# 512 columns per matmul in the down products of the first two feed-forward layers

## The reference

```python
def conv_ffn(h, w_in, dw, w_out):
    u = causal_dwconv(h @ w_in, dw)
    gate, val = u[..., :D_FF], u[..., D_FF:]
    return (jax.nn.silu(gate) * val) @ w_out      # D_FF = 2816
...
x = x + conv_ffn(rmsnorm(x, norm_ffn_g[layer]), ffn_w_in[layer], ffn_dw[layer], ffn_w_out[layer])
```

## Time and profile before

| | |
|---|---|
| median of three runs | 2604.6 us |
| the profiled execution | 2604.33 us, of which the span of the trace is 2602.5 us |
| granted TensorE clock, mean of the span | 0.986 |
| PE busy | 2506.9 us (96%), 25266 matmuls |
| PEld busy | 2367.6 us (91%), 25266 weight loads |
| DVE, ACT, POOL busy | 52%, 43%, 38% |

### The profile page before, as it was taken

One profiled execution on the slowest core, in us unless ns is written; L12 is line 12 of the kernel. 1 busy time (PEld: TensorE's weight loads), 2 busy tenths in 40 slices (PEclk: granted clock), 3 DMA queues, 4 the chain that ended last, 5 costly groups with the idle time before them and its releaser, 6 DMA issues.

```text
span 2602.5 us, 62231 instructions
## 1 busy us (share of the span) xinstructions
PE 2506.9 (96%) x25266; PEld 2367.6 (91%) x25266; DVE 1340.9 (52%) x2035; ACT 1122.6 (43%) x1652; POOL 995.2 (38%) x488
## 2 busy tenths in 40 slices
PE   6999898999999999998999999999999999999998
PEld 6888796997999999977989999999998769999998
DVE  7657554613477741798533677612143344455521
ACT  7834455454444433334534344433244444444422
POOL 3324220461444444325322444444443104444442
PEclk8899999999999999999999999999999999999999
DMA  4221001251232233323212322233222103322232
GB/s 147 74 65 59 2 1 63 82 194 38 94 97 95 91 102 100 130 65 105 90 65 65 97 94 91 92 111 114 88 93 69 49 1 97 97 89 97 96 99 74
DMA packets 62180, 219.43 MB, mean 84 GB/s; under 512 B 6752, under 2 KB 9184, under 8 KB 61408
## 3 DMA queue, kind: packets, MB, share of 16 engines
q1 hardware_dynamic: 58880, 207.76, 24.4%
q10 hardware_dynamic: 3168, 9.75, 1.1%
HBM read 213.29 MB, written 4.19 MB: 84 GB/s over the span
## 4 chain that ended last, share of the span: by engine, by line
PE 83%; DVE 8%; issue 6%; ACT 2%; POOL 1%; DMA 0%; DVEq 0%; POOLq 0%; ACTq 0%
PE psum L571 70%; DVE psum L2698 5%; PE psum L713 3%; PE psum L721 2%; PE psum L1072 1%; PE psum L1021 1%; PE psum L1251 1%; POOL wl L520 1%; PE psum L1290 1%; DVE psum L2267 1%; PE psum L1253 0%; ACT wh L1382 0%; PE psum L683 0%; PE psum L1278 0%; PE psum L690 0%
## 5 line engine op out<-in xcount | busy, mean ns | idle before, releaser
L520 POOL TENSOR_TENSOR wl<-raw,wh 128x1024 fp32r<-128x1024 f32 x388 | 949.0, 2455 | 1464.0 <-ACT wh L1382 1463.6
L571 PE MATMUL psum<-acth,wh 128*128 128x256 f32 x3792 | 763.8, 283 | 20.6 <-DVE actl L2789 8.2
L571 PE MATMUL psum<-actl,wh 128*128 128x256 f32 x3792 | 753.9, 281 | 0.0
L571 PE MATMUL psum<-acth,wl 128*128 128x256 f32 x3792 | 753.3, 280 | 0.0
L1382 ACT ACTIVATE wh<-raw 128x1024 fp32r<-128x1024 f32 x388 | 407.1, 1056 | 625.1 <-PE psum L571 601.4
L571 PEld LDWEIGHTS psum<-acth,wh 128*128 128x128 f32 x3792 | 582.7, 189 | 38.1 <-issue 30.2
L571 PEld LDWEIGHTS psum<-acth,wl 128*128 128x128 f32 x3792 | 581.7, 189 | 0.0
L571 PEld LDWEIGHTS psum<-actl,wh 128*128 128x128 f32 x3792 | 581.5, 189 | 0.0
L2628 DVE TENSOR_TENSOR cu<-psum,rstd 128x512 f32<-128x512 f32 x132 | 91.1, 690 | 236.9 <-PE psum L571 219.6
L571 PE MATMUL psum<-hidh,wh 128*128 128x256 f32 x1056 | 210.0, 277 | 0.0
L571 PE MATMUL psum<-hidh,wl 128*128 128x256 f32 x1056 | 209.5, 277 | 0.0
(11 more groups left out here) (442 smaller groups left out, 4048.3 us busy)
## 6 DMA issues: line engine op xcount, KB each, us to landing
raw<-in_weights SPq DMA_DIRECT2D x388, 512.0 KB, 3.3
xt<-in_x SPq DMA_DIRECT2D x4, 512.0 KB, 5.4
xt<-in_x ACTq DMA_DIRECT2D x1, 2048.0 KB, 9.3
out_x<-xt SPq DMA_DIRECT2D x6, 256.0 KB, 2.3
mem<-in_mem ACTq DMA_DIRECT2D x1, 1024.0 KB, 11.0
memn<-memh ACTq DMA_DIRECT2D x1, 1024.0 KB, 7.0
memn<-meml ACTq DMA_DIRECT2D x1, 1024.0 KB, 10.0
memh<-memn ACTq DMA_DIRECT2D x1, 1024.0 KB, 4.7
```

Of the source, the lines that this page charges most:

```text
L520: pool.tensor_tensor(wl[:, s, :], raw[:, s, :], wh[:, s, :].bitcast(F32), ALU.subtract).then_inc(split_done, 1)
L571: ins = pe.matmul(out[:, n:n + HALF], w, m[:, n:n + HALF], start=first and n == 0, stop=last and n + HALF >= out.shape[1])
```

## The change

`product` gets the parameter `width`, 256 unless given, in place of the constant HALF. `down` gives width=T, so each pair of operands is one matmul of 512 columns instead of two of 256. Nothing else is changed: same blocks, order, banks, waits and slots. `dense`, `tile` and `last_down` keep 256.

```diff
-            def product(out, slot, b, hi, lo, start, stop, rows=slice(0, P)):
+            def product(out, slot, b, hi, lo, start, stop, rows=slice(0, P), width=HALF):
 
                 w_h, w_l = wh[rows, slot, b * P:(b + 1) * P], wl[rows, slot, b * P:(b + 1) * P]
                 for w, m, first, last in ((w_h, hi, start, False), (w_h, lo, False, False), (w_l, hi, False, stop)):
-                    for n in range(0, out.shape[1], HALF):
-                        ins = pe.matmul(out[:, n:n + HALF], w, m[:, n:n + HALF], start=first and n == 0,
-                                        stop=last and n + HALF >= out.shape[1])
+                    for n in range(0, out.shape[1], width):
+                        ins = pe.matmul(out[:, n:n + width], w, m[:, n:n + width], start=first and n == 0,
+                                        stop=last and n + width >= out.shape[1])
                 return ins
...
                             mm = product(bank[(t0 + s) % 4][:, :], (u0 + j) % SLOTS, k % BLOCKS,
-                                         hi[:, k, :], lo[:, k, :], k == 0, k == FT - 1)
+                                         hi[:, k, :], lo[:, k, :], k == 0, k == FT - 1, width=T)
```

## The result

The changed kernel is slower: 2616.1 us against 2605.8 (medians of 13 runs each), a ratio of 1.0032 with a 95% interval from 1.0019 to 1.0045. The two medians differ by 10.3 us; the ratio, which uses all the runs, stands for about 8 us, with 5 to 12 inside the interval. The profiled execution took 2611.83 us, with a span of 2610.0, which is 7.5 us more than before.

The account below looks back on a forecast made before the run. The prediction took TensorE to bound the kernel, busy 96% of the span. Its one term, 1056 x (226.7 ns minus the 512-column step), came to 0 against the profiled 2604.33 us, giving 2604.5 us, range 2593 to 2608.5.

Parts of the forecast that it names:

- TensorE sets the span: Whole kernel: PE busy 96% of the span, 83% of the last chain, so its pace reaches the end nearly undiminished.
- Nothing waited differently: Down products: slot and bank are still released when the last column is through, which is the same column.
- the slots and POOL kept up: Down products: POOL, with 57.5 us of work in 119.6, would keep up even with a stage 10 us shorter.
- the clock stayed at 1.00: Down products: the granted clock stays at 1.00, the 2.4 GHz level; otherwise the forecast is wrong.
- The stages right before and behind kept their steps: Stages around the down products: they keep 256 columns and their pace, unchanged to the tenth of a microsecond.
- PEld's busy time: Down products: the weight loads' busy time falls by half without any gain in the span.
- the price of a 512-column matmul: Down products: excess goes with columns, so 512 columns step in 226.7 ns; the term 1056 x 0 is 0, chance 0.66.
- rival 2: Down products: late hand-over between long matmuls at every step, +6.7 us, to 2611.3 us; chance 0.10.
- The bound that I allowed: Down products: upper bound on the 512-column step, 233 ns from L1254 in the attention, 6.7 us slower.
- a weight load which is not hidden: Third layer's attention: such a load lies in the 256- and 512-column forms alike and drops out of their difference.
- Rival 1: Down products: a fixed time per instruction, halved by the change; 7.0 us saved (2597.6) or 10.6 (2594.0); chance 0.24.
- The formula: Down products: a warm gap of N / 2.4 + 2.5 ns, 215.8 ns at 512 columns, would give 11.5 us; not built on.

Follow-up runs that it names:

- e10_all_moved: The changed kernel (512 columns in both down products) with every SBUF buffer, weights included, 64 bytes higher: 2613.8 us, the kernel before 2604.7 beside it.
- e11_weights_moved: The changed kernel with wh and wl 64 bytes higher and all behind them 128 bytes higher: 2654.2 us, the kernel before 2604.7 beside it.
- e13_act_d192: The kernel before, 256 columns throughout, with par placed before acth so acth and actl lie at distance 192 from wh: 2597.4 us, ratio 0.9969.
- e9_all_512_moved: The kernel before with 512 columns in every product that has them and 96 bytes free behind xt and rstd: 2633.0 us, ratio 1.011.

## Why the prediction was wrong

**What held.** TensorE sets the span: 7.0 us of the two stages came out as 7.5 of the span. Nothing waited differently, the slots and POOL kept up, the clock stayed at 1.00. The stages right before and behind kept their steps. Some farther off did not: the stage on memh that took 33.79 us took 35.05 (113.3 and 117.8 ns), the second of 384 matmuls on headh 43.95 in place of 45.63 (117.8 and 113.3 ns). Such shifts nearly cancel over the kernel, so it is in part luck that the span grew by so nearly what the two stages did. And PEld's busy time did not fall by half: its loads of 188 ns had overlapped one another and now lie apart.

**The step that failed** is the price of a 512-column matmul, the one term of the sum. From the attention I took what 256 further columns cost, 0.228 us for two matmuls or 114 ns each, read it as the same 0.443 ns per column that the down product pays, and so came to 226.7 ns there. But in the down product the further 256 columns cost 120.0 ns, from 113.3 to 233.3, and the term was not 0 but 1056 x 6.6 ns = 7.0 us. The increment isn't a property of the matmul: in the table it is 106.7 ns at distance 0, 116.6 at 32 and 120.0 at 192. The base differed between the two places as well. L1254 takes 0.12 us at 256 columns in rows 5, where the down product steps in 0.113, and I used that only to discount rival 2. By the sizes of the buffers the attention's operands lie at distance 0, where the table has 120.0 ns at 256 columns.

The bound that I allowed, 233 ns from L1254 at 512 columns in rows 6, is what the changed kernel does. That is partly luck, as this matmul lies at another distance: 0 modulo 512, where no steady stream was run, while the streams at 256 modulo 512 step in 226.7. Why it takes 0.23 us is open.

That a weight load which is not hidden drops out of the difference was sound. It is L1253's own, ahead of it; the next one runs beside L1253's columns (PEld in the kernel before; the bracket is idle time ahead and what ended it):

```profile
2056.02 0.19 PEld L1253 LDWEIGHTS psum<-cumh,hybr 128*128 128x128 f32 x1 [0.76 <-issue]
2056.13 0.19 PEld L1254 LDWEIGHTS psum<-cuml,hybr 128*128 128x128 f32 x1
```

**Rival 2** gave 6.7 us and its sign, and was right in size; its mechanism, a late hand-over between long matmuls, is not what the runs show. In bfloat16 the same hand-over leaves 2.5 ns, and at another distance to the weights the float32r one steps in 226.7. With a chance of 0.10 and its time, 2611.3, left outside the range, it was undervalued against a row that showed it.

**Rival 1**, a fixed time per instruction, is nearly what holds at distance 0: 13.3 ns of excess at 256 columns and 13.3 at 512, so that halving the instructions gains. At distance 192 it is 6.7 (11.1 at the slower pace) and 20.0. The question "per instruction or per column" had no answer independent of the layout, and I didn't have the thought to ask for it, although the rows of acth (116.7) and hidh (113.3) differed with the same operation.

**The formula** of the Trainium skill's page "TensorE: Matmul & The Clock Gate", section "Back-to-back issue gap", which the page gives for a single matmul by itself, makes 215.8 ns of 512 columns. The bfloat16 form side by side meets it even in a steady stream (215.9), and float32r doesn't at any distance tried.

## What to carry to other kernels

Before changing the width of a float32r matmul, look at where its moving operand lies relative to the weights, modulo 256 bytes: at a distance of 0 (always 256 modulo 512 here) one matmul of 512 took 226.7 ns against 240.0 for two of 256. At 192 it took 233.3 against 226.7 for two of 256 at their faster pace and 235.6 at their slower; at 32 it took the same 233.3 as two at the faster pace. So the best that two of 256 do equals the best of 512, but no run here could choose the pace. Price an instruction from a steady stream of its own kind with the same layout; a slope from one place and a base from another don't add up. And when a long stretch ahead of a loop is shortened, look whether packets of instructions now arrive inside the loop.

## What the runs showed of the hardware

The place of two buffers relative to each other changes the pace of float32r matmuls by up to 6%: 113.3 to 120.0 ns at 256 columns, 226.7 to 233.3 at 512. A collision in SBUF between the reads of the moving operand and the weight load beside it would explain the dependence on the distance, and is an inference; what the memory does was not seen, and it doesn't by itself explain the two paces. The Trainium skill's page "SBUF — State Buffer", section "SBUF: two separate sides", holds that within the engine side only the pair of ports that VectorE and GpSimd share causes contention. e10_all_moved and e11_weights_moved, 123.20 and 119.71 us for the same 528 matmuls, show a cost between TensorE's own two operands that this sentence leaves no room for, if the inference is right.

At 256 columns two paces exist for one layout (e13_act_d192: 113.3 and 117.8 ns in the two down products), and at 512 a small second one showed too (e9_all_512_moved: 233.3 ns in the first two layers' down products, 232.4 in the third's). The spread of the kernel's runs may come from this; that wasn't tested.
